# One core, one encoder block: VectorE left alone with the scan, skew transfers spread, ssm weight loads ahead of y's stores, v in two buffers, first x tiles eight at a time

## What is computed

```python
hn = rms_norm(h, norm1_g)
q, k, v, u, g_na, g_ssm = split(hn @ w_in)          # 1024 each for q, k, v, u; 2048 each for the gates
y_na  = neighbourhood_attention(q, k, v, rpb) @ w_proj_na      # 16 heads of 64
y_ssm = s5_branch(u, ...) @ w_proj_ssm              # two complex scans, 64 groups, 64 states
h = h + (sigmoid(g_na) * y_na + sigmoid(g_ssm) * y_ssm) @ w_out
h = h + conv_gated_ffn(rms_norm(h, norm2_g), w_up, conv_w, conv_b, w_down)
out = rms_norm(h, final_g)[meta:]
```

## Time and profile before

| | |
|---|---|
| median of three runs | 1544.02 us |
| the profiled execution | 1545.01 us, its span 1543.3 us |
| TensorE matmul, busy | 1477.8 us (96%) |
| VectorE | 564.4 us (37%) |
| ScalarE | 692.5 us (45%) |
| GpSimd | 1038.8 us (67%) |
| mean granted TensorE clock | 0.984 |
| moved by DMA | 277.09 MB, mean 180 GB/s |

### The profile page before, as it was taken

One profiled execution on the slowest core, in us unless ns is written; L12 is line 12 of the kernel. 1 busy time (PEld: TensorE's weight loads), 2 busy tenths in 40 slices (PEclk: granted clock), 3 DMA queues, 4 the chain that ended last, 5 costly groups with the idle time before them and its releaser, 6 DMA issues.

```text
span 1543.3 us, 31379 instructions
## 1 busy us (share of the span) xinstructions
PE 1477.8 (96%) x11825; PEld 1400.3 (91%) x11825; DVE 564.4 (37%) x1140; ACT 692.5 (45%) x916; POOL 1038.8 (67%) x490
## 2 busy tenths in 40 slices
PE   6898898899989999999999999999999999999998
PEld 5898898898879999999999999999999998888886
DVE  3474688887636323442222222222222222003002
ACT  4544443232145445444454554555554554334434
POOL 3400005775368857888778888888888888888885
PEclk9899999999989999999999999999999999999999
DMA  7797544554457645575555556556555556565553
GB/s 231 223 199 195 159 148 150 170 173 130 126 168 225 199 135 164 178 238 187 164 164 183 185 177 190 178 177 190 180 178 187 186 177 207 178 189 189 185 188 134
DMA packets 251258, 277.09 MB, mean 180 GB/s; under 512 B 30748, under 2 KB 237948, under 8 KB 250540
## 3 DMA queue, kind: packets, MB, share of 16 engines
q1 hardware_dynamic: 224864, 250.58, 53.6%
q10 hardware_dynamic: 26252, 25.35, 5.4%
q0 software_dynamic: 64, 0.07, 0.0%
HBM read 263.32 MB, written 12.39 MB: 179 GB/s over the span
## 4 chain that ended last, share of the span: by engine, by line
PE 78%; DVE 10%; ACT 3%; issue 2%; DVEq 2%; ACTq 2%; SPq 1%; DMA 1%; POOL 0%
PE ps L1476 19%; PE ps L1478 19%; PE ps L1477 19%; PE ps L1819 5%; PE ps L1818 5%; PE ps L1820 5%; DVE ps L1010 3%; DVE scan_states L1200 2%; DVEq L1199 1%; PE ps L1676 1%; ACT w_hi L458 1%; DVE w_lo L462 1%; ACTq L750 1%; DMA w_raw<-in_w_in 1%; SPq L409 1%
## 5 line engine op out<-in xcount | busy, mean ns | idle before, releaser
L462 POOL TENSOR_TENSOR w_lo<-w_raw,w_hi 128x1024 fp32r<-128x1024 f32 x420 | 1008.6, 2413 | 466.9 <-ACT w_hi L458 298.9
L458 ACT ACTIVATE w_hi<-w_raw 128x1024 fp32r<-128x1024 f32 x464 | 488.8, 1059 | 741.9 <-PE ps L1478 509.1
L1476 PE MATMUL ps<-act_hi,w_hi 128*128 128x258 f32 (+2 forms) x2432 | 701.4, 288 | 29.6 <-POOL w_lo L462 23.1
L1478 PE MATMUL ps<-act_hi,w_lo 128*128 128x258 f32 (+2 forms) x2432 | 695.4, 286 | 0.0
L1477 PE MATMUL ps<-act_lo,w_hi 128*128 128x258 f32 (+2 forms) x2432 | 694.2, 285 | 0.0
L1476 PEld LDWEIGHTS ps<-act_hi,w_hi 128*128 128x128 f32 x2432 | 466.7, 192 | 36.7 <-issue 18.1
L1477 PEld LDWEIGHTS ps<-act_lo,w_hi 128*128 128x128 f32 x2432 | 467.5, 192 | 0.0
L1478 PEld LDWEIGHTS ps<-act_hi,w_lo 128*128 128x128 f32 x2432 | 465.5, 191 | 0.0
L1818 PE MATMUL ps<-w_hi,hidden_hi 128*128 128x512 f32 x352 | 139.2, 395 | 0.0
L1819 PE MATMUL ps<-w_hi,hidden_lo 128*128 128x512 f32 x352 | 139.0, 395 | 0.0
L1820 PE MATMUL ps<-w_lo,hidden_hi 128*128 128x512 f32 x352 | 139.0, 395 | 0.0
(11 more groups left out here) (251 smaller groups left out, 1563.9 us busy)
## 6 DMA issues: line engine op xcount, KB each, us to landing
w_raw<-in_w_up SPq DMA_DIRECT2D x176, 512.0 KB, 3.5
w_raw<-in_w_in SPq DMA_DIRECT2D x128, 512.0 KB, 4.3
w_raw<-in_w_down SPq DMA_DIRECT2D x88, 512.0 KB, 4.0
w_raw<-in_w_out SPq DMA_DIRECT2D x32, 512.0 KB, 3.5
w_raw<-in_w_proj_na SPq DMA_DIRECT2D x16, 512.0 KB, 3.4
w_raw<-in_w_proj_ssm SPq DMA_DIRECT2D x16, 512.0 KB, 3.5
bias_rows<-skew_scratch ACTq DMA_DIRECT2D x32, 128.0 KB
w_raw<-in_w_glu SPq DMA_DIRECT2D x8, 512.0 KB, 3.5
```

The source lines that it names most:

```text
L458: act.activation(slot(whi, k), slot(raw, k), ACT.Copy).then_inc(s_hi, 1)
L462: pool.tensor_tensor(slot(wlo, k), slot(raw, k), slot(whi, k).bitcast(F), ALU.subtract).then_inc(s_lo, 1)
L1476: mm(o, slot(whi, k)[:, cols], xh[:, kt, lo:lo + n], start=kt == 0, stop=False)
L1478: ins = mm(o, slot(wlo, k)[:, cols], xh[:, kt, lo:lo + n], start=False, stop=kt == units * UKT - 1)
```

## The change

* Start: TensorE does twelve products of ones before anything is loaded and two after the sixth tile. The tiles use four banks; six are transposed ahead, two more between the halves of the first unit, the rest as before. w_hi 0 stands behind tile 0, 1 behind 4, 2 behind 8, then 9, 11, 13; the token squares are spread between tiles and units. x0T lies elsewhere, so u need not wait for the spill, which is issued after the square root.
* GpSimd splits twelve units instead of eight at the start, and q unit 51.
* b is loaded and transposed before c. c is loaded in whole rows to `craw` (in the place of the u chunks) and paired by a copy on GpSimd; SP's u chunk loads wait for that.
* v has two staging buffers with a semaphore each.
* q and the first 24 gate units are copied by ScalarE without the scale. The scale of q (times 1/8) is transposed to a column `qsc` and multiplied in at the scores, in two instructions; the gates are scaled by VectorE during attention. VectorE does nothing but the scan in this phase. `g_make(1)` stands behind the scan, and the rest two tiles ahead instead of three.
* The 64 skew transfers go one or two behind each k unit, one behind each q unit and each of the first 24 gate units.
* ssm: the outputs of a tile stand behind the first half of the next unit, the next kernels behind the outputs. SP issues y's stores and loads, the bias and q, k, v loads of the first two pairs, each behind the load of a unit of weights.
* The meta scores stand behind the first attention unit.

```diff
+        vst = (at("v_stage_a", 29696, [P, 4, CB]), at("v_stage_b", 25600, [P, 4, CB]))
+        x0T = at("x_feature_major", 52736, [P, KT, L])
...
+            for u in range(16):
+                load_in(U_K, HALF, u // 8, (u % 8,))
+                for c in range(3 * u // 2, 3 * (u + 1) // 2):
+                    skew(c)
+            for u in range(16):
+                load_in(U_Q, 0, u // 8, (u % 8,))
+                skew(24 + u)
...
+            for t in range(KH):
+                load_in(U_G, 4 * HALF, 4, (t,))
+                y_store(t)
+                if t:
+                    y_load(t - 1)
+                if t == 5:
...
+                    bias_load(sp, 0)
+                    att_load(sp, 0)
...
+            unit_behind = {0: 0, 4: 1, 8: 2, 9: 3, 11: 4, 13: 5}
...
+            def q_copy(n):
+                act.wait_ge(s_used, U_Q + 4 * (n + 1))
+                act.wait_ge(s_kst[n % 2], 32 * (n // 2 + 2))
...
+            def gate_copy(n):
+                act.wait_ge(s_used, U_G + 4 * (n + 1))
+                banks = 2 * ((n + 1) % 2)
+                act.activation(gate_na[:, 2 * n:2 * n + 2, :], ps[:, banks:banks + 2, 0:NL], ACT.Copy).then_inc(s_ga, 1)
...
-            for n in range(4 + G_SCAN):
-                for c in range(min(SCAN_STEPS * n, NCH - 1), min(SCAN_STEPS * (n + 1), NCH - 1)):
-                    scan_step(c)
...
-                if n < 4:
-                    kq_block(4 + n, LIVE, 2, qm, 2 * ((n + 1) % 2))
...
+            for c in range(NCH - 1):
+                scan_step(c)
+            dve.nop().then_inc(s_scan, 1)
...
+                for t in range(2):
+                    dve.scalar_tensor_tensor(out=S[:, t:4:2, :], in0=ps[:, 0:2, WK * t:WK * (t + 1)], scalar=qsc[:, t:t + 1],
+                                             in1=bm[:, t:4:2, :], op0=ALU.mult, op1=ALU.add)
...
+            def idle_passes(n):
+                for _ in range(n):
+                    mm(ps[:, 3, 0:P], ones[:, :], ones[:, :], start=True, stop=True)
+
+            pe.wait_ge(s_const, 1)
+            idle_passes(12)
...
+            for t in range(KH):
+                if t + 1 < KH:
+                    gate_half(t + 1, 0)
+                if t == 0:
+                    pe.wait_ge(s_scan, 1)
+                chunk_out(t)
                 if t + 1 < KH:
                     kernels(t + 1)
+                    if t == 3:
+                        pe.wait_ge(s_g, 1 + SEED)
+                    gate_half(t + 1, 1)
```

416 lines of the change are left out of this document (218 added, 198 removed).

## The result

The changed kernel takes 1509.1 us by the median of four runs (1506.2 to 1512.6), the kernel before 1543.4 us beside it: a ratio of 0.977, 95% interval 0.975 to 0.979. It is 2.3% faster. The forecast was 1489.0 us in a range of 1480 to 1508 us: the sign was right, and the time lies 1.1 us above the range. The profiled execution took 1508.4 us with a span of 1506.7 us, 36.6 us less than before, where the sum said 55.0.

What follows compares the result with a forecast made beforehand. TensorE, busy 96% of the span, was taken as the bound, so only its waits and lower clock could be gained. Terms summed to 55.0 us off 1545.0: 1490.0 profiled, 1489.0 by the median, range 1480 to 1508 us.

Steps and rivals of the forecast that it cites:

- q and gates: Joined q and gate phase: ScalarE copying the blocks itself removes waits for w_lo and gate_na; gain 20.0 us, bounds 15 and 20.
- End of v, start of k: Waits for a staged v block and w_tr: spread skew transfers and two v buffers give back 7.9 us.
- "transfers" term: Loads in the first 130 us: little room on the DMA engines, 2 us charged, bounds 0 and 15.
- The start: Start to u's twelfth unit: earlier first matmul and spread token squares, 16.3 us gained less 1.5 charged, 14.8 forecast.
- GpSimd takes four more low halves ...: nothing: Start: four more low halves on GpSimd, with three extra one-column transposes, were put at no cost.
- The pace of 0.78 us per tile: Start: remaining ten tiles, in turns of VectorE and ScalarE, laid out at 0.78 us of VectorE each.
- the clock charge: Start: idle matmuls may not hold TensorE's clock from 8 to 13 us; 1.5 us charged, bounds 0 and 3.
- the charge: ssm stage: VectorE needs 7.0 to 7.2 us per tile against TensorE's 6.9; 2.5 us charged, net -0.9.
- Start of attention: Last ssm output to second scores: moving work off ScalarE's queue removes waits and clock loss; gain 11.8 us, bounds 7 and 12.
- SP takes these over: 4.4 + 0.4 + 0.5 us per tile: Start of attention: SP's issuing per tile, about 10 us in tiles 5 and 6, against TensorE's 7.1; lag covered.
- SP is the slow place: Rival: at 1.19 us per issue a tile takes SP 10.4 us; +28 us, 1517 us; chance 0.06 if still faster.
- lie in stretches where VectorE is under 60% busy: nothing: Three extra scalings, scores in two instructions and gate_na in attention, 0.7 us each, were put at no cost.

Runs made afterwards that it cites:

- the two experiments: Changed kernel with VectorE copying q and gate blocks between scan steps again: 1522.9 us; the same with the second g_make ahead of the scan: 1529.3 us.
- 1.3 us by the experiment: Changed kernel with GpSimd making eight low halves at the start, not twelve, VectorE making units 8 to 11: 1510.8 us, ratio 0.977.
- the experiment gives 4.2: Changed kernel with VectorE scaling gate_na in attention before it waits for and copies the gate block: 1504.1 us, ratio 0.974.

## Why the forecast was wrong, point by point

**q and gates, right.** 20.5 us against 20.0, no wait for w_lo or gate_na. The scan ends with the strip at 326.8 us, TensorE asks for it at 329.5: 2.7 us of cover where 2.3 were forecast. Scan steps stay 1.72 us with a split beside them. But that ScalarE stands behind q_meta was only part of the reason: by the two experiments the copies are 14.5 us and VectorE's start up to 7.6.

**End of v, start of k, right, and better.** The w_tr wait is 1.4 us (1.5 forecast). With the "transfers" term of 2 us, which did not come (DMA share 0.83), the stretch gained 8.2. The k stage gained 1.6 and not 3.4: the clock's loss there did not all go (0.93 from 141 to 165 us).

**The start, 5.0 us too much.** The step that failed is "GpSimd takes four more low halves ...: nothing". They made GpSimd busy while VectorE's small copies ran (2.49 us for a copy of one row), and TensorE stopped: 1.3 us by the experiment. The lower clock from 51 to 54 us, behind this stop, is 1.5 us more. It is partly chance: of the profiles with the stop, three kept the clock up. The pace of 0.78 us per tile gave an end of the fourth unit at 31.4 us, 32.9 with the clock charge; it was 34.4. The reason was wrong too: TensorE's own transposes, 0.5 us per tile, had not been counted, and they carry most of the pace. About 0.7 us lie in the next four units, most of it around the three small products. GpSimd's copy of c, put at nothing, took 1.89 us and no wait of TensorE goes with it.

**ssm, 5.4 us too much, 3.9 of it real.** The difference is the half unit of gates that changed sides. VectorE's "7.0 to 7.2 us" per tile was about right; TensorE's own 6.9 is 7.1 by the run without splits. The step that failed is the charge: of bounds 0 to 6, 2.5 was taken, for two engines that need the same time per tile. What was left out is that a queue with no slack passes each wait on: the gate block's wait of 1.37 us became 2.17 us at TensorE, and the stops cost clock as well (0.97). The loss of 4.8 us, counted alike, lies just past the net of -4.4 at the end of the bound.

**Start of attention, 5.2 us too much, counted alike 6.7.** The step that failed is "SP takes these over: 4.4 + 0.4 + 0.5 us per tile". In tiles 1 to 6 it was so (4.3 to 4.8 us). At the last two, with bias rows and q, k, v in the same queue, issuing the eight stores took 6.75 and 10.9 us, and the v tail and the weight behind the first of them and the bias landed 9.6 and 11.9 us after their issue. The forecast had no term for a late landing. Where it comes from is only in part shown: y rows and bias fill a quarter of the engines, but no run separates the two. The rival "SP is the slow place" had this mechanism, with the price per issue right (0.84 and 1.36 us against 1.19), but spread over the whole stage, not at its end. By that rival's own price of 10.4 us a tile, two tiles would have been an estimate of 12 us more of SP, of which 7 are covered: 5 us.

**Attention, 5.4 us too much.** The step that failed is "lie in stretches where VectorE is under 60% busy: nothing". A mean share says nothing of the place. VectorE idled some 7 us ahead of the gate block and not at all behind it, and the scaling was put behind. Five of the six pairs with the scaling took 0.7 to 1.1 us longer, 4.1 us together; the experiment gives 4.2. The other 1.3 us of the row are in the first pair and belong to the thin stretch.

**The range.** Four terms were some 4 to 7 us short each, all on the same side, and only two of them (ssm 6, start of attention 7) had a bound that nearly reached there. Three of the four (start, ssm, attention) have one root: VectorE was slowed or given work at a place where the next thing in its queue was due, though its mean share had room.

## What to carry to other kernels

An added instruction is free only if idle time stands between it and the next thing that someone waits for; look in the timeline of one period at what is behind it in its queue, not at the engine's share. Put it ahead of the longest wait of the period. A transfer that runs on few of the DMA engines holds what is queued behind it for longer than its bytes say. Look at what moves while the DMA share is low, and start the last such transfers before a deadline early, where an idle queue allows it. And where several edits push work onto one engine, the errors of their estimates have the same sign, so the range must be wider than each alone asks.

## What the runs showed of the hardware

A VectorE instruction between SBUF operands that meets a GpSimd split waits until that split ends and then takes its own time: copies of 0.2 us took 2.32 and 2.49, multiplications of 0.68 us 1.92 to 2.96, the scaling of 0.7 us 1.44 and 2.36; each of these ended 0.1 to 0.6 us behind a split, which takes 2.4 alone. It is not only instructions of two SBUF inputs, as in the forecast; the copies have one. The scan, with an operand in PSUM, kept its 1.72 us per step. The Trainium skill states the same in "SBUF — State Buffer", section SBUF: two separate sides: an exclusive lock held for a whole instruction, taken by VectorE's fast copies too; the trace agrees, and with the split's 2.4 us as the price the ssm bound could have been set.

For 8 us the DMA engines stood at a share of 0.28 and 91 GB/s in the mean, first with the bias of two pairs and the ends of a weight and of v, then with a y tile in rows of 272 bytes. The weight among them landed after 11.9 us where 4.1 is the median.
